# Lower parts of the last two token tiles of a router: from VectorE to GpSimd, and one clock product less

## What is computed

```
xt = rms_norm(x, ln_ffn[layer])                     # 512 x 1024
grp_prob = softmax(xt @ w_rg + b_rg)                # 4 groups, the best one is taken
exp_logits = (xt @ w_re + b_re)[chosen group]       # 8 experts of that group
exp_p, exp_idx = top_k(softmax(exp_logits), 2)
gates = grp_p * exp_p / sum(exp_p)
y[token] += gate * (silu(xb @ w_gate[e]) * (xb @ w_up[e])) @ w_down[e]    # 32 experts
```

## Time and profile before

| | us |
|---|---|
| runs of the kernel | 1717.71, 1713.36, 1717.56 |
| median | 1717.56 |
| profiled execution, its own time | 1716.05 |
| its span, first to last instruction | 1714.3 |
| PE busy in the span | 1673.0 |
| DVE busy | 675.1 |
| ACT busy | 418.3 |
| POOL busy | 218.5 |

### The profile page before, as it was taken

How to read it: one execution, slowest core, us unless ns; L and a number is a source line. 1 busy time by engine, 2 the same in 40 slices (tenths; PEclk the granted TensorE clock), 3 DMA queues, 4 the chain that set the end, 5 groups by cost and what they waited for, 6 DMA issues and landing times.

```text
span 1714.3 us, 23355 instructions
## 1 busy us (share of the span) xinstructions
PE 1673.0 (98%) x9467; PEld 1092.6 (64%) x9467; DVE 675.1 (39%) x1210; ACT 418.3 (24%) x804; POOL 218.5 (13%) x152
## 2 busy tenths in 40 slices
PE   7999999999999999998999999999999999999997
PEld 7877888654545454545888888888754544545453
DVE  3877763622423333234413123132623332323233
ACT  4466653210101101013332323223410010101110
POOL 1500001100000000001544243342100000000000
PEclk9999999999999999999999999999999999999999
DMA  9410202799999999996222122122499999999995
GB/s 202 103 50 1 63 40 99 277 430 426 427 425 428 419 427 425 426 426 259 71 76 99 49 99 98 54 94 99 197 408 421 425 425 422 426 421 424 421 425 243
DMA packets 67868, 460.67 MB, mean 269 GB/s; under 512 B 5568, under 2 KB 31392, under 8 KB 42432
## 3 DMA queue, kind: packets, MB, share of 16 engines
q1 hardware_dynamic: 67040, 457.01, 65.5%
q0 software_dynamic: 736, 2.34, 1.1%
HBM read 457.24 MB, written 2.10 MB: 268 GB/s over the span
## 4 chain that ended last, share of the span: by engine, by line
PE 88%; DVE 4%; DMA 4%; issue 2%; ACT 1%; SPq 0%; DVEq 0%; ACTq 0%
PE bank L153 31%; PE bank L1807 24%; PE bank L1822 12%; PE bank L1781 7%; PE bank L1829 5%; DMA ring<-in_w_up_dram 3%; DVE X L2088 2%; PE bank L2312 1%; DMA ring<-in_w_in_odd_dram 1%; PE bank L1816 1%; PE bank L940 1%; PE bank L953 1%; DMA ring<-in_w_in_even_dram 1%; PE bank L1504 0%; PE bank L956 0%
## 5 line engine op out<-in xcount | busy, mean ns | idle before, releaser
L1807 PE MATMUL bank<-ring,SCR 128*64 128x512 f32 x2048 | 446.4, 592 | 2.6 <-DMA ring<-in_w_up_dram 2.6
L153 PE MATMUL bank<-ring_r 128*128 128x512 f32 (+2 forms) x1216 | 359.4, 377 | 1.2 <-DVE ring_r L401 0.9
L1807 PEld LDWEIGHTS bank<-ring,SCR 128*64 128x64 f32 x2048 | 157.5, 137 | 283.2 <-issue 282.8
L153 PEld LDWEIGHTS bank<-ring_r 128*128 128x128 f32 x1216 | 225.1, 191 | 42.7 <-issue 2.2
L2243 POOL TENSOR_TENSOR ring_r<-ring,ring_r 128x1024 fp32r<-128x1024 f32 x62 | 150.8, 2470 | 685.2 <-DVE ring_r L2243 460.3
L1822 PE MATMUL bank<-ring,SCR 128*64 128x512 f32 x1024 | 226.8, 595 | 9.4 <-DVE X L2088 9.4
L2088 DVE TENSOR_TENSOR X<-X,bank 128x512 f32<-128x512 f32 x240 | 148.1, 680 | 94.7 <-PE bank L1829 94.7
L1822 PEld LDWEIGHTS bank<-ring,SCR 128*64 128x64 f32 x1024 | 76.8, 137 | 139.1 <-issue 130.8
L1841 DVE SCALAR_TENSOR_TENSOR SCR<-SCR,bank 128x512 f32<-128x512 f32 x32 | 23.9, 747 | 345.2 <-PE bank L1807 345.2
L153 PE MATMUL bank<-ring_r,SCR_r 128*128 128x512 f32 x576 | 138.7, 395 | 0.0
L1829 PE MATMUL bank<-SCR_r 128*128 128x512 f32 x512 | 132.4, 400 | 1.1 <-DVE SCR_r L1838 1.1
(11 more groups left out here) (420 smaller groups left out, 1599.1 us busy)
## 6 DMA issues: line engine op xcount, KB each, us to landing
ring<-in_w_gate_dram SPq DMA_DIRECT2D x64, 2048.0 KB, 13.7
ring<-in_w_up_dram SPq DMA_DIRECT2D x64, 2048.0 KB, 16.9
ring<-in_w_down_dram SPq DMA_DIRECT2D x64, 2048.0 KB, 13.4
ring<-in_w_in_odd_dram SPq DMA_DIRECT2D x8, 2048.0 KB, 9.7
ring<-in_w_in_even_dram SPq DMA_DIRECT2D x16, 512.0 KB, 6.7
ring<-in_w_in_odd_dram SPq DMA_DIRECT2D x8, 1024.0 KB, 7.8
ring<-in_w_out_odd_dram SPq DMA_DIRECT2D x4, 2048.0 KB, 8.5
X<-in_x_dram SPq DMA_DIRECT2D x4, 512.0 KB, 5.5
```

What stands on the lines that cost most here:

```text
L153: mm = pe.matmul(out, lhs[a], rhs[b], start=(first and i == 0), stop=(last and i == 2))
L1807: mm = pe.matmul(bank[SLOTS * u:SLOTS * u + SLOTS, :], xt[:, k, SLOTS * u:SLOTS * u + SLOTS], w[u][:, k, :], start=(k == 0), stop=(k == KT ...
```

## The change

The lower parts of tiles 2 and 3 are made by POOL, in two instructions each: XN = X·rstd (L1577 after the change), then XN_r = XN − XNU (L1579). POOL's router stream is a new function, `router_pool`, in which tile 3's rstd stands behind tile 2's lower part. VectorE keeps the lower parts of tiles 0 and 1. The second half of the gathers waits for the new semaphore `xn_lower_pool`: for tile 2 at its start, for tile 3 ahead of its fourth product. The clock product ahead of tile 3's logits is left out; the other one stays. Both layers are changed alike.

```diff
@@ -1432,7 +1432,7 @@
 
 
         ROUTE = dict(m_route_pe=("logits0", "logits1", "logits2", "counts_first", "logits3", "counts"), m_route_dve=("gain", "masks_first", "oh_first", "gdiff", "ediff", "masks", "routed"))
-        PER_LAYER = dict(rexp=3, xn_upper=NT, xn_lower=NT,
+        PER_LAYER = dict(rexp=3, xn_upper=NT, xn_lower=2, xn_lower_pool=2,
                          oh=PAIRS // 2, **dict.fromkeys(("ohg", "ot", "ot_out", "gs_out", "gate", "up", "sil", "hh", "ht", "ht_out"), PAIRS),
                          **dict.fromkeys(("gat", "xt_out", "y", "y_upper", "y_lower"), NE),
                          **dict.fromkeys(("comb", "added"), 8 * PAIRS))
@@ -1521,7 +1521,6 @@
                 logits_pe(pe, l, 2, range(4))
                 raw_pe(pe, l, 3)
                 logits_pe(pe, l, 2, range(4, KT))
-                keep_clock(pe, 1, PB[0])
                 counts_first(pe, l)
                 logits_pe(pe, l, 3)
 
@@ -1561,15 +1560,23 @@
             dve.wait_ge(gcol_in, 16)
             dve.tensor_tensor(WR[:, :, :], WR[:, :, :], gcol[:, l, :, None].to_broadcast([P, KT, NR]), ALU.mult).then_inc(moe_sem(l, "gain"), 1)
 
+        def lower_of(eng, t):
+            return eng.scalar_tensor_tensor(by_ktile(XN_r[:, t, :]), by_column(X[:, t, :]), rstd[:, t:t + 1], by_ktile(XNU[:, t, :].bitcast(F32)),
+                                            ALU.mult, ALU.subtract)
+
         def lower_dve(dve, l, t):
             dve.wait_ge(*moe_wait(l, "xn_upper", t + 1))
-            dve.scalar_tensor_tensor(by_ktile(XN_r[:, t, :]), by_column(X[:, t, :]), rstd[:, t:t + 1], by_ktile(XNU[:, t, :].bitcast(F32)),
-                                     ALU.mult, ALU.subtract).then_inc(moe_sem(l, "xn_lower"), 1)
-
-        def lower_half(dve, t, a):
-            ks = slice(4 * a, 4 * a + 4)
-            return dve.scalar_tensor_tensor(by_ktile(XN_r[:, t, :])[:, ks, :], by_column(X[:, t, :])[:, ks, :], rstd[:, t:t + 1],
-                                            by_ktile(XNU[:, t, :].bitcast(F32))[:, ks, :], ALU.mult, ALU.subtract)
+            lower_of(dve, t).then_inc(moe_sem(l, "xn_lower"), 1)
+
+        def router_pool(pool, l, step):
+
+            norm_pool(pool, 2 * l + 1, step, (0, 1))
+            for t in (2, 3):
+                norm_pool(pool, 2 * l + 1, step, (t,))
+                pool.wait_ge(rstd_done, NT * (2 * l + 1) + t + 1)
+                step.then(pool.tensor_scalar(by_ktile(XN[:, t, :]), by_column(X[:, t, :]), rstd[:, t:t + 1], None, ALU.mult))
+                pool.wait_ge(*moe_wait(l, "xn_upper", t + 1))
+                pool.tensor_tensor(XN_r[:, t, :], XN[:, t, :], XNU[:, t, :].bitcast(F32), ALU.subtract).then_inc(moe_sem(l, "xn_lower_pool"), 1)
 
         chosen = {}
 
@@ -1581,9 +1588,9 @@
                     second_choice(dve, l, step, HEAD_T, *chosen[l])
                     dve.wait_ge(resid, (R_EVEN, R_ODD)[l])
                 raw_out(dve, dve.tensor_copy, l, t, 1).then_inc(tr_out_d, 1)
-                if n != 6:
-                    lower_dve(dve, l, min(t, 2))
-                else:
+                if t < 2:
+                    lower_dve(dve, l, t)
+                if n == 6:
                     logits_dve(dve, l, step, 0)
                     logits_dve(dve, l, step, 1)
                     first_choice(dve, l, step, HEAD_T)
@@ -1717,8 +1724,6 @@
             dve.wait_ge(*mw("masks_first", 1))
             positions(dve, step, HEAD_T, PB[7][:, 0:2 * NE])
             ones_first(dve, HEAD_T).then_inc(ms("oh_first"), 1)
-            dve.wait_ge(*mw("xn_upper", NT))
-            lower_half(dve, NT - 1, 0)
             logits_dve(dve, l, step, 3)
             first_choice(dve, l, step, TAIL_T)
             second_choice(dve, l, step, TAIL_T, *second_gaps(dve, l, step, TAIL_T))
@@ -1950,9 +1955,9 @@
                 down(i)
 
             pe.wait_ge(*mw("oh", 1))
-            pe.wait_ge(*mw("xn_lower", NT - 1))
+            pe.wait_ge(*mw("xn_lower_pool", 1))
             for q in range(4):
-                gather_mm(pe, FIRST_BANKS[q], (2 * q, 2 * q + 1), DUO, range(2, NT), mw("xn_lower", NT) if q == 2 else None).then_inc(ms("gat"), 1)
+                gather_mm(pe, FIRST_BANKS[q], (2 * q, 2 * q + 1), DUO, range(2, NT), mw("xn_lower_pool", 2) if q == 0 else None).then_inc(ms("gat"), 1)
             pairs_loop(pe, pair)
             for n, m in enumerate(LAST_ORDER):
                 pe.wait_ge(*mw("y_lower", 2 * last + 1 + m % 2))
@@ -2117,7 +2122,6 @@
                 y_out(i)
 
             ones_first(dve, TAIL_T).then_inc(ms("oh"), 1)
-            lower_half(dve, NT - 1, 1).then_inc(ms("xn_lower"), 1)
             for q in range(4):
                 x_out(q, FIRST_BANKS[q], 0, q)
             gates_dve(dve, l, step)
@@ -2604,7 +2608,7 @@
                 pool.dma_start(gcol[:, :, :], ln_ffn.rearrange("l (p k) -> p l k", p=P)).then_inc(gcol_in, 16)
             gdn_pool(pool, step)
             if upto > 1:
-                norm_pool(pool, 1, step)
+                router_pool(pool, 0, step)
                 pool.wait_ge(*moe_wait(0, "logits3", 1))
                 pool.dma_start(SCR[:, CO_AT:SCR_N], const_odd).then_inc(odd_in, 16)
             if upto > 2:
@@ -2616,7 +2620,7 @@
                 norm_pool(pool, 2, step)
                 ret_pool(pool, step)
             if upto > 3:
-                norm_pool(pool, 3, step)
+                router_pool(pool, 1, step)
 
         @block.scalar
         def _(act):
```

## The result

| | before | after |
|---|---|---|
| median of 6 runs each, us | 1715.56 | 1723.98 |
| ratio, 95% interval | | 1.0051 [1.0041, 1.0061] |
| span of the profiled execution | 1714.3 | 1720.7 |
| POOL busy | 218.5 | 244.1 |

The change costs 0.51%, 8.4 us between the medians. Three more runs of the kernel before have brought its median from the 1717.56 of three runs to 1715.56. Before the routers the two kernels are the same, so each layer is read from its own start: VectorE's addition that ends tile 2 starts at 306.31 and 1210.80 before, at 304.21 and 1214.45 after. The 2.10 us by which the profiled execution of after is ahead there are not the work of the change. From there to the same point of the second layer it loses 5.75 us, and 2.75 more to the end: 8.5, as the medians say (8.4).

The account below looks back on a forecast made before the run. VectorE's chain was taken to set the start of the last gathers, which bounds each layer. +2.9 us in the first layer, about 0.2 hidden, and +2.9 in the second gave 1717.56 + 5.6 = 1723.2 us; range 1715.8 to 1728.5.

Parts of the forecast that it names:

- The sum: Both layers: +2.9 us in the first, about 0.2 of it hidden, and +2.9 in the second; 5.6 us slower.
- Step 4, the head: Router head, tile 2: POOL's subtraction stalls VectorE's two-operand L1650; chain 2.2 us later, last add 2.0, TensorE idles nearly 2.
- Step 3, the product: POOL's X·rstd for tiles 2 and 3: taken as 2.4 us each, bounds 1.2 and 4.0.
- Tile 3's part of step 4: Router tail: one-hots wait for POOL's product, L1650 for its subtraction; masks and last gathers 2.9 us later.
- rival (c): Clock falls after TensorE's idle time; half speed in the last 32 gathers, 2.0 us a layer, 1727.2 us; chance 0.15.
- nothing can hide in the second layer: Second layer's last pair: no delay hides in TensorE's 1.86 us wait for weights, so all +2.9 us arrives.
- the wait of 0.57: First layer's last pair, TensorE waiting for weights: about 0.2 us of the 2.9 us delay hides there.
- Rival (a): VectorE's operations slip past POOL's, free help: gains 1.1 us in the second layer, about 0.2 in the first; chance 0.14.
- rival (d): POOL's product takes 4.0 us, delaying the second layer's head chain too: 10.6 us in all, 1728.2 us; chance 0.10.
- Step 1: Removing the clock product ahead of the last logits saves TensorE 0.54 us and alone brings those logits forward by 0.54.

Follow-up runs that it names:

- e7: Kernel before with one more VectorE operation, 2.06 us, ahead of the head's last add into X, POOL untouched; 1727.54 us, ratio 1.0064.
- e11: Kernel before with the same extra 2.06 us on VectorE as e7, plus three clock products in TensorE's idle time; 1719.71 us, ratio 1.0029.
- e3: Changed kernel with three clock products ahead of tile 3's transposes, filling TensorE's idle time; 1721.41 us, ratio 1.0030 to the kernel before.
- e2: Kernel before, only without the clock product ahead of tile 3's logits; 1717.03 us, ratio 1.0006.
- e1: Changed kernel with the removed clock product put back behind tile 2's logits; 1727.25 us, ratio 1.0060 to the kernel before.
- e6: Changed kernel with POOL's product reading X and writing XN without a step, from wrong columns; 1722.87 us, ratio 1.0046 to the kernel before.
- e10: e9 without the clock product ahead of tile 3's logits; 1715.62 us, ratio 1.0000 to the kernel before.
- e9: Against the kernel before: POOL makes only the products, VectorE subtracts both tiles late, half ahead of the tail's counts, clock product kept; 1714.99 us, ratio 0.9998.

## Why the prediction was right, and where it was not

The forecast of 1723.2 us stands beside 1723.98, and "slower" came true; but that the two times are so near is luck. The sum said +5.6 us, and the change costs 8.4. It was added to 1717.56, the median of three runs, and that was 2.0 us above the 1715.56 of six; the base was too high by most of what the sum was too low.

- **Step 4, the head: right.** A two-operand operation stands until POOL's subtraction ends (2.38 us), the last add is 1.90 late, TensorE idles 1.87. The earlier trace rows were enough for it. The stall met later operations than the one named, L1663 in the first layer and L1687 in the second. The Trainium skill (SBUF — State Buffer, Who interferes with whom) has the rule that a VectorE instruction with two SBUF inputs contends with a GpSimd instruction that reads SBUF, and the trace agrees for the subtraction. The Trainium skill (SBUF — State Buffer, SBUF: two separate sides) says "for the whole instruction", and there the one-input product differs: it let the one-hots pass after 2.0 of 3.9 us. The measurement decides.
- **Step 3, the product: the size was off.** 3.9 to 4.1 us against 2.4 taken; the upper bound, 4.0, was the value. The Trainium skill (GPSIMD Engine Reference, Performance pitfalls for Q7 kernels) led to an estimate of 2.5, too low by 1.4 to 1.6; its share for the step, half as much again, is 1.37 to 1.43 here (3.9 and 4.1 over 2.85 and 2.86).
- **Tile 3's part of step 4: wrong in its mechanism.** It had the one-hots wait for the product's end; they were not held at all in the first layer and 0.5 us in the second. The masks came 3.78 late in the first layer, where the sum had 2.9, since tile 3's logits were themselves late and no longer at full clock.
- **The step that failed is the clock.** The sum had it at nothing; it stood as rival (c) with 0.15 and 2.0 us a layer, placed in the last 32 gathers. The clock fell with TensorE's idle time, 13 to 16 us before those, and slowed transposes, logits, counts and the first gathers; the last gathers ran at full clock. e7 against e11 prices it at 3 us a layer, on top of a delay of 2.4. In the change itself e3, with its head at full clock, has +2.91 and +4.15 at the gates in place of +6.21 and +4.79: the first is about what the sum had, though its first gathers ran in part at half clock; the second shows that idle time in the tail costs as well.
- **That nothing can hide in the second layer was wrong, and there it offset the clock.** Of 4.79 us at the gates 2.75 reach the end, near the forecast's 2.9; the wait for weights at the last pair was most of the cover (1.86 before, 0.23 after). In the first layer nothing offset it: 5.75 of 6.21 arrive, where the sum had 2.7, and the wait of 0.57 in which 0.2 was to hide did not shrink but is 2.24 after. So the second layer was right by two errors, and the first was short by half.
- **Rival (a), free help, is refuted; rival (d), the slow product of 10.6 us, had the product's length but not its effect.** In the second layer its 3.94 us let the head's chain pass until the subtraction came, and the last add is 1.91 us late, not 3.6. Step 1's 0.54 us for the clock product is the start of the next row, which was itself stretched; e2 measures 0.80, and no gain from it.

## What to carry to other kernels

Before giving GpSimd a piece of VectorE's work, list the two-operand VectorE operations in that stretch and ask who waits for the chain they are in: a 2.4 us instruction on GpSimd stopped a chain for up to its whole length wherever it was put. Then ask what TensorE does meanwhile: a delay of 2 us in a stretch of small products set the gates back by 5.5 to 7.1 us where TensorE stood idle in it, and by 2.4 where it was kept busy. Work to keep the clock belongs into the wait, not behind it (e3 and e1). And before a forecast is believed for its time, compare the difference that it claims: a base of three runs was off here by 2 us, a quarter of the effect.

## What the runs showed of the chip that was not expected

- A one-input GpSimd product of 128x1024 stops two-operand VectorE operations for its first 2.0 us with a step of eight columns and 1.0 us without, of 3.9 and 2.85 us, and lets them pass for its last 1.9 in every case here; it is itself stretched (to 4.64 and 5.45 us) where such a VectorE operation was running first.
- The granted clock fell at quite different delays behind like idle times: in the change within the idle time of 1.87 us (0.57 already in 312 to 313), in e6, with the same 1.87 us, some 2 us behind its end (0.80 in 316 to 317, 0.50 from 317). It fell with 0.74 us in e2, and stayed with 0.63 in e10 and 1.03 in e9. What sets this is left open.
- Half clock lasted although TensorE was busy without a break: 13 us in the change's first layer, 12 us busy of 12. The transposes ahead of the odd layer were spared it in the timeline of PE after the change: they take 2.00 us behind an idle time of 1.63, with the clock at 1.00, where the earlier trace rows have 3.03 behind 2.79, with the clock at 0.50 in a part of them.

```profile
805.98 2.00 PE L342 MATMUL bank<-CE,X 128*128 128x128 f32 x16 [1.63 <-DVE X L2098]
```
